# A three-layer f32 network on one core: the last block's mixer changed from column-major to row-major projections, with its entry norm, head norms, rotation and gates rebuilt around that

## What is computed

```python
x = rms_norm(x, final_norm_g)                                   # end of the first block
mod = silu(c) @ w_ada + b_ada                                   # six rows of 1024
shift_m, scale_m, gate_m, shift_f, scale_f, gate_f = split(mod)
h = _rms(x) * (1 + scale_m) + shift_m
proj = h @ w_in     # fq fk fv fog (512 columns each), forget logits (8), rq rk rv rg (512 each)
fq, fk = _rms(fq) * q_gain, _rms(fk) * k_gain                   # by head, 8 heads of 64
fox = softmax(fq fk^T / 8 + cum[t] - cum[s], causal) @ fv       # cum: running sum of log_sigmoid(forget)
fox = _rms(fox) * fox_gain * sigmoid(fog)
rq, rk = _rope(rq), _rope(rk)                                   # 4 heads of 128
ret = (rq rk^T * decay) @ rv
ret = _rms(ret) * ret_gain * silu(rg)
x = x + gate_m * (concat(fox, ret) @ w_out)
h = _rms(x) * (1 + scale_f) + shift_f
x = x + gate_f * (square(relu(h @ w_mlp_in)) @ w_mlp_out)
```

## Time and profile before

| | us |
|---|---|
| median of 3 runs (1222.89 to 1227.58) | 1227.35 |
| the profiled execution | 1228.55 |
| its span | 1226.7 |
| PE busy (95% of the span) | 1167.2 |
| DVE busy (59%) | 720.6 |
| ACT busy (43%) | 525.3 |
| mean granted TensorE clock, share of full | 0.963 |

### The profile page before, as it was taken

How to read it: one execution, slowest core, us unless ns; L and a number is a source line. 1 busy time by engine, 2 the same in 40 slices (tenths; PEclk the granted TensorE clock), 3 DMA queues, 4 the chain that set the end, 5 groups by cost and what they waited for, 6 DMA issues and landing times.

```text
span 1226.7 us, 16582 instructions
## 1 busy us (share of the span) xinstructions
PE 1167.2 (95%) x7264; PEld 1044.9 (85%) x7264; DVE 720.6 (59%) x675; ACT 525.3 (43%) x578; POOL 43.9 (4%) x85
## 2 busy tenths in 40 slices
PE   6988999999999999999999999959989989999998
PEld 4977799898998999989888998849866877898997
DVE  4654465497666776665367667664335566745544
ACT  5544364353544453344454443434332334544441
POOL 2200000000000000000000000010000000000000
PEclk9989899999999999999999999968979889999999
DMA  9832454357577555555447577633122202454540
GB/s 358 311 141 82 152 182 164 136 189 294 211 285 289 212 220 178 201 178 183 167 161 294 215 275 277 235 105 138 70 103 103 69 35 103 173 206 171 188 155 35
DMA packets 31463, 222.12 MB, mean 181 GB/s; under 512 B 3628, under 2 KB 3920, under 8 KB 6688
## 3 DMA queue, kind: packets, MB, share of 16 engines
q1 hardware_dynamic: 26640, 188.03, 42.0%
q0 software_dynamic: 4224, 31.88, 7.2%
q10 hardware_dynamic: 528, 1.16, 0.3%
HBM read 220.01 MB, written 1.05 MB: 180 GB/s over the span
## 4 chain that ended last, share of the span: by engine, by line
PE 87%; DVE 6%; ACT 4%; issue 1%; POOL 0%; DMA 0%; POOLq 0%; ACTq 0%; DVEq 0%
PE ps L426 40%; PE ps L441 38%; ACT hi L968 2%; DVE lo L1382 2%; PE ps L501 1%; PE ps L819 1%; PE ps L816 1%; PE ps L559 1%; PE ps L549 1%; DVE hn L1422 1%; ACT hn L994 1%; PE ps L784 1%; PE ps L665 1%; PE ps L686 1%; DVE work L1857 1%
## 5 line engine op out<-in xcount | busy, mean ns | idle before, releaser
L1382 DVE TENSOR_TENSOR lo<-raw,hi 128x2048 fp32r<-128x2048 f32 x175 | 400.5, 2290 | 246.5 <-ACT hi L968 246.3
L968 ACT ACTIVATE hi<-raw 128x2048 fp32r<-128x2048 f32 x175 | 334.4, 1912 | 360.5 <-PE ps L426 175.1
L426 PE MATMUL ps<-xt_hi,hi 128*128 128x256 f32 x1280 | 367.4, 287 | 6.0 <-DVE xt_lo L1432 6.0
L426 PE MATMUL ps<-xt_hi,lo 128*128 128x256 f32 x1280 | 365.6, 286 | 0.0
L426 PE MATMUL ps<-xt_lo,hi 128*128 128x256 f32 x1280 | 365.4, 285 | 0.0
L426 PEld LDWEIGHTS ps<-xt_hi,hi 128*128 128x128 f32 x1280 | 249.4, 195 | 7.2 <-issue 6.6
L426 PEld LDWEIGHTS ps<-xt_hi,lo 128*128 128x128 f32 x1280 | 249.3, 195 | 0.8 <-issue 0.2
L426 PEld LDWEIGHTS ps<-xt_lo,hi 128*128 128x128 f32 x1280 | 249.1, 195 | 0.0
L441 PE MATMUL ps<-hi,yt_hi 128*128 128x512 f32 x544 | 214.7, 395 | 1.8 <-DVE yt_lo L1628 1.4
L441 PE MATMUL ps<-lo,yt_hi 128*128 128x512 f32 x544 | 212.3, 390 | 0.0
L441 PE MATMUL ps<-hi,yt_lo 128*128 128x512 f32 x544 | 212.3, 390 | 0.0
(11 more groups left out here) (228 smaller groups left out, 1158.1 us busy)
## 6 DMA issues: line engine op xcount, KB each, us to landing
raw<-in_weights SPq DMA_DIRECT2D x176, 1024.0 KB, 5.0
work<-in_w_ada POOLq DMA_DIRECT2D x16, 1536.0 KB, 6.8
work<-in_gains POOLq DMA_DIRECT2D x6, 512.0 KB, 4.1
work<-in_gains ACTq DMA_DIRECT2D x2, 512.0 KB, 7.2
h<-in_x SPq DMA_DIRECT2D x2, 512.0 KB, 6.1
work<-in_mem POOLq DMA_DIRECT2D x2, 512.0 KB, 8.6
work<-in_pool SPq DMA_DIRECT2D x1, 1024.0 KB, 16.4
out_y<-h SPq DMA_DIRECT2D x4, 256.0 KB, 2.0
```

What stands on the lines that cost most here:

```text
L426: mm = pe.matmul(o, ws[:, slot, k, j * P:(j + 1) * P], xs[:, c, :], start=(c == 0 and n == 0 and j % 2 == 0), stop=(c == KC - 1 and n == 2 ...
L968: act.activation(hi[:, p % RING], raw[:, p % RING], ACT.Copy).then_inc(hi_ready, 1)
L1382: dve.tensor_tensor(lo[:, p % RING], raw[:, p % RING], hi[:, p % RING].bitcast(F32), ALU.subtract)\
```

## The change

It reorders the units (fk ahead of fq) and makes all eight projections `unit_x`.

- **Entry norm.** Per tile: add, `gained` (h times the final gain) and `gained_scaled` (times `scale_m`) on DVE, squares of both `h` and the gained row on ACT, five POOL instructions for two roots, and one DVE step by halves (`mix2_rows`) that gives the modulated norm straight from them. The final-normed `h` is written later by ACT. Transposes and `fk` go by tile.
- **Head norms.** ACT squares from the PSUM bank, DVE sums along the row (128x512 to 8 or 4 values), POOL adds eps and raises to -1/2, DVE multiplies the bank by it. The softmax is not divided: the row total enters the eps of the fo norm instead.
- **Forget gate.** 24 matmuls of 256 columns with a padded 128-column weight; the running sum goes as a 65th feature into `k_aug`, against a 65th feature of ones in `q_aug`. Both are then transposed by PE (32 transposes, 65 rows out) and copied.
- **Scores.** One f32 matmul on 65 partitions a head and half of the queries, and then the mask; six groups instead of four. Values come out with rows on the partitions.
- **Rotation.** DVE multiplies by tables of cos, sin and -sin from the bank (four instructions a tile); PE then transposes rq and rk (16).
- **Gates.** ACT's Sigmoid and Silu; `foxg` and `retg` are multiplied into the weights of `out2` when those are split (four instructions a half on ACT and DVE).
- **Rows of mod.** Two transposes of 24 rows (`mod_turn`), a store to DRAM and six loads that repeat a row over the partitions, on POOL's queue.
- **mlp2's norm.** DVE multiplies by `scale_f` ahead of the root and does the rest in one instruction.

"late" is a new 4096-column tile in the place of `mt_hi` and `mt_lo`.

```diff
+    ("fk", _blocks("in2", [1])),
     ("fq", _blocks("in2", [0])),
-    ("fk", _blocks("in2", [1])),
...
+    k_aug, q_aug = late[:, 0:1040], late[:, 1040:2080]
...
-        def row(name, index, first):
-            for j in range(2):
-                o = claim(first + j, ("row", name, j))
-                for k in range(HC):
-                    m = index * KC + j * HC + k
-                    mm = pe.matmul(o[:, k * P:(k + 1) * P],
-                                   mod[:, m:m + 1].to_broadcast((P, P)), ident[:, :],
-                                   start=True, stop=True, skip_group_check=True)
-                filled_by(mm, ("row", name, j))
+        def mod_turn(n, b):
+            def run():
+                pe.wait_ge(*mod_ready.at(n))
+                o = claim(b, ("mod", n))
+                filled_by(pe.transpose(o[0:24, 0:P], mod[:, 24 * n:24 * n + 24], ident[:, :]), ("mod", n))
...
-        transposes("mix2", 0)
-        transposes("mix2", 1)
-        unit_w(UNIT["fq"], XT, (0, 1), split("mix2"))
...
-        head_back("fq", hn[:, 0, :])
...
+        turn_mix2(0)
+        unit_x(UNIT["fk"], XT, (0, 1), "mix2", {(0, 1): lambda: turn_mix2(1)})
...
+        for c in range(KC):
+            for n, (xs, ws) in enumerate(((xt_hi, ff_hi), (xt_hi, ff_lo), (xt_lo, ff_hi))):
+                mm = pe.matmul(o[:, 0:S], ws[:, 8 * c:8 * c + P], xs[:, c, :], start=(c == 0 and n == 0),
+                               stop=(c == KC - 1 and n == 2), skip_group_check=True)
...
+        unit_x(UNIT["fq"], XT, (2, 3), hooks={(1, 0): forget_turned, (1, 1): forget_sums})
...
+                    o = claim(b + i, ("aug", x, t, i))
+                    for k in range(4):
+                        mm = pe.transpose(o[0:65, k * P:(k + 1) * P], src[:, t, 4 * i + k, :], ident[:, :])
+                    filled_by(mm, ("aug", x, t, i))
...
+        unit_x(UNIT["fv"], XT, (0, 1), hooks={(0, 1): aug_turned("fk", k_aug, 0, 4), (1, 0): aug_turned("fk", k_aug, 1, 6),
+                                              (1, 1): aug_turned("fq", q_aug, 0, 4)})
+        aug_turned("fq", q_aug, 1, 6)()
...
-                    pe.matmul(o, fq_t[r, c, qt * P:(qt + 1) * P], fk_t[r, c, 0:nk], start=True, stop=False,
-                              skip_group_check=True)
-                    pe.matmul(o, ident[0:8, 2 * c + b:2 * c + b + 1].to_broadcast((8, P)), cum_rows[:, 0:nk],
-                              start=False, stop=False, skip_group_check=True)
-                    mm = pe.matmul(p[:, a * S + qt * P:a * S + (qt + 1) * P], ident_bf[:, :],
-                                   mask_bf[:, :], start=False, stop=True, skip_group_check=True)
...
-        rotated("q", rq_t, "rq")
...
+                for i, hd in enumerate(heads):
+                    pe.matmul(o[:, i * nk:(i + 1) * nk], fq_t[0:65, hd, qt * P:(qt + 1) * P], fk_t[0:65, hd, 0:nk],
+                              start=(i == 0), stop=False, skip_group_check=True)
+                for i, hd in enumerate(heads):
+                    mm = pe.matmul(o[:, i * nk + qt * P:(i + 1) * nk], ident_bf[:, :], mask_bf[:, :],
+                                   start=False, stop=True, skip_group_check=True)
...
+        unit_x(UNIT["rq"], XT, (2, 3), hooks={(0, 0): together(fox_scores(0, 4), fox_scores(1, 5)),
+                                              (0, 1): together(fox_scores(2, 6), fox_scores(3, 7)),
+                                              (1, 1): together(fox_scores(4, 4), fox_scores(5, 5))})
...
+        unit_x(UNIT["rk"], XT, (0, 1), hooks={(0, 0): together(fox_turned(0, 6), fox_turned(1, 7)),
+                                              (1, 0): together(fox_values(0, 4), fox_turned(2, 6), fox_turned(3, 7)),
+                                              (1, 1): fox_turned(4, 5)})
...
+        unit_x(UNIT["rv"], XT, (2, 3), hooks={(0, 0): fox_turned(5, 6), (0, 1): fox_values(1, 7), (1, 0): mod_turn(1, 6),
+                                              (1, 1): together(*rq_turned)})
...
+        unit_x(UNIT["fog"], XT, (0, 1), hooks={(0, 1): together(*rk_turned), (1, 0): together(ret_scores(0), ret_scores(1)),
+                                               (1, 1): together(ret_scores(2), ret_scores(3))})
...
+        unit_x(UNIT["rg"], XT, (2, 3), hooks={(0, 1): together(ret_values(0, 4), ret_values(1, 5)),
+                                              (1, 0): mixed_turned["fo", 0], (1, 1): mixed_turned["fo", 1]})
...
-        pair(UNIT["out2"], ((yt_ready.at("fo"),), (yt_ready.at("ro"),)),
-             {(0, 1, 0): lambda: row("gate_m", 2, 6), (0, 1, 1): scale_f,
-              (1, 0, 0): lambda: row("shift_f", 3, 6), (1, 1, 0): lambda: row("gate_f", 5, 4),
...
+        pair(UNIT["out2"], ((read(("mixed", "fo", 0)), read(("mixed", "fo", 1))), ()),
+             {(0, 0, 1): mixed_turned["ro", 0], (0, 1, 0): mixed_turned["ro", 1],
+              (1, 0, 0): late_heads(0), (1, 0, 1): late_heads(1),
...
+            if ORDER[p][0] - UNIT["out2"] in (0, 1):
+                gains = "retg" if ORDER[p][1] else "foxg"
+                for k in range(HC):
+                    ins = act.activation(hi[:, p % RING, k], raw[:, p % RING, k], ACT.Copy, scale=col(gains, k))
...
+            act.activation(late[:, n * NB:(n + 1) * NB], src, ACT.Square, scale=1.0 / 32,
+                           accum_out=fin[:, c:c + 1]).then_inc(*fin_sq.up((x, t, b)))
...
+            act.activation(squares_of(x, t), bank(label), ACT.Square, scale=width ** -0.5)\
+                .then_inc(*head_squared.up((x, t)))
...
+            if n == "mlp2":
+                ins = dve.scalar_tensor_tensor(hn[:, t, :], hn[:, t, :], rstd[:, c:c + 1], shift_f_row,
+                                               ALU.mult, ALU.add)
...
+        def gained(t, b):
+            blk = slice(b * NB, (b + 1) * NB)
+            dve.wait_ge(*read(("u", UNIT["mlp1"] + 14 + b, t)))
+            dve.tensor_tensor(hgn[:, t, blk], h[:, t, blk], gain[:, blk], ALU.mult).then_inc(*hg_ready.up((t, b)))
+        def gained_scaled(t):
+            for b in range(2):
+                dve.wait_ge(*hg_ready.at((t, b)))
+            dve.tensor_tensor(hn[:, t, :], hgn[:, t, :], scale_row, ALU.mult).then_inc(*hs_ready.up(t))
+        def mix2_rows(t):
+            dve.wait_ge(*hs_ready.at(t))
+            dve.wait_ge(*fin_r.at(("2", t)))
+            for b in range(2):
+                blk = slice(b * NB, (b + 1) * NB)
+                dve.scalar_tensor_tensor(hn[:, t, blk], hn[:, t, blk], rstd[:, 16 + t:17 + t], shift_row[:, blk],
+                                         ALU.mult, ALU.add).then_inc(*xn_ready.up((t, b)))
         u = UNIT["mlp1"] + 14
...
+            add_residual(u, b, 0)
+            gained(0, b)
+        gained_scaled(0)
         add_residual(u, 0, 1)
+        gained(1, 0)
+        mix2_rows(0)
         add_residual(u, 1, 1)
-        for j in range(2):
-            dve.wait_ge(*read(("row", "scale_m", j)))
-            dve.wait_ge(*read(("row", "shift_m", j)))
-        scaled_row("mix2", 0, h)
...
+            dve.tensor_reduce(mean_sq[:, 8 * n:8 * n + c], cut(squares_of(x, t), c), AX_X, ALU.add)\
+                .then_inc(*head_mean.up((x, t)))
...
+            r = head_r[:, 8 * n:8 * n + c].rearrange("p (a b) -> p a b", b=1).to_broadcast((P, c, NB // c))
+            dve.tensor_tensor(dst, cut(bank(label), c), r, ALU.mult).then_inc(*free(label))
...
+            cos = cos_m[:, t:t + 1, :].to_broadcast((P, 8, 64))
...
-        step(dve.reciprocal(fog_t, fog_t))
...
-        step(dve.reciprocal(rg_exp_t, rg_exp_t))
...
+            gp.tensor_tensor(r, m, power[:, :].to_broadcast((P, c)), ALU.pow).then_inc(*head_root.up((x, t)))
...
+        def final_roots(t):
...
+            gp.tensor_tensor(rstd[:, 14 + t:15 + t], v1, power[:, :], ALU.pow).then_inc(*fin_r.up(("1", t)))
+            gp.wait_ge(*fin_step.at(("a", t)))
+            gp.wait_ge(*fin_sq.at(("g", t, 1)))
+            gp.tensor_tensor(v2, v2, fin[:, 4 * t + 3:4 * t + 4], ALU.add).then_inc(*fin_step.up(("v2", t)))
+            gp.wait_ge(*fin_step.at(("v2", t)))
+            gp.tensor_tensor(rstd[:, 16 + t:17 + t], v2, power[:, :], ALU.pow).then_inc(*fin_r.up(("2", t)))
...
+        gp.wait_ge(mod_stored, 32)
+        gp.dma_start(scale_f_row, mod_row(4)).then_inc(loaded["scale_f"], 16)
+        gp.dma_start(shift_f_row, mod_row(3)).then_inc(loaded["shift_f"], 16)
+        gp.dma_start(gate_f_row, mod_row(5)).then_inc(loaded["gate_f"], 16)
```

955 lines of the change are left out of this document (544 added, 411 removed).

## The result

The changed kernel takes **1132.88 us** (median of 4 runs, 1132.57 to 1133.13), the kernel before, beside it on the same chip, 1225.87. The ratio is 0.924, with a 95% interval of 0.922 to 0.927: 93.0 us less. What came true is nearly to the number the rival that had been given 10% ("all doors in time and no slow clock", 1135).

The account below looks back on a forecast made before the run. The prediction took PE as the bound, with its work, clock and waits. Savings of 36.1 work, 21.2 idle, 22.6 clock and 2 outside the stage sum to 81.9: 1227.35 - 81.9 = 1145.5 us, range 1134 to 1161.

Parts of the forecast that it names:

- all doors in time and no slow clock: First rival listed, 10%: idle 3.5 us, half clock 1 us, second row's cover not missed, 1135 us.
- The work of PE: In the changed stage, PE's work at full clock falls from 177.5 to 141.4 us, by 36.1.
- the lower of its two bounds: 65-row score matmul taken at 0.22 and 0.43 us; the upper bound, 0.41 and 0.62, would add 3.0 us.
- The clock's term: In the changed stage, the half clock's cost falls from 28.6 to 6 us, giving back 22.6.
- perhaps two stretches behind values and scores at 1.7 each: Half-clock loss kept in the changed stage behind values and scores, part of the 6 us kept.
- The waits' term: In the changed stage, PE's idle time falls from 28.7 to 7.5 us, by 21.2; 3.5 stays at the entry.
- three doors and the hand-overs: Idle of 4 us behind the entry: `forget_turned` 0.5, `pair(out2)` 1.1, rows of mod 1, some loss at each hand-over.
- the second covered the chain from the add to the transposes, ... so up to 1.7 comes back as a wait: In the cross attention, two rows removed save 3.4 us of work, but up to 1.7 returns as waiting: gain 2.
- DVE as the bound in bursts: Rival, 20%: DVE holds back units and hooks in the stage, 8 + 4.6 us over the forecast, 1158 us.
- the 1.5 us named as the mark of being wrong: Sign against the forecast: POOL's root of eight values taking over 1.5 us in the profile.
- the clock would not recover: Rival, 7%: low clock follows transposes and f32 pieces, so 20 of the 22.6 us are lost, 1166 us.
- the slower case at 1281: Rival, 2%: pieces put into every unit keep the clock at half through the whole stage, 1281 us.

Follow-up runs that it names:

- score_split: The changed kernel with its 65-row score matmul split into 64 rows and one row, each head's mask behind them, head after head: 1158.93 us.
- before_filled: The kernel before with dummy bf16 matmuls in TensorE's nine waits in the mixer stage: 1218.05 us, ratio 0.992.
- before_grouped: The kernel before with each group's score matmuls ordered by kind (64 rows, then 8 rows, then masks): 1214.09 us, ratio 0.989.
- after_holes: The changed kernel with five waits of about 2 us put into TensorE, at the start of rq, rk, rv, fog and rg: 1143.59 us.
- score_alternate: The changed kernel with each mask set right behind its head's 65-row score matmul, instead of scores first and then masks: 1136.35 us.
- dve_plus2: The changed kernel with sixteen dummy reductions on DVE, two at a time at eight places from fk to the end of rg: 1145.69 us.
- score_split_grouped: The changed kernel with score matmuls split into 64 rows and one row, ordered by kind across heads, then the masks: 1148.00 us.

## Why the prediction was right, and where it fell short

**The work of PE was right.** 36.1 forecast, 35.8 measured. The 65-row score matmul was taken at the lower of its two bounds, 0.22 and 0.43 us, and that held. The timeline of PE, two groups of two heads with 256 keys, answers to the earlier trace rows:

```profile
844.96 1.03 PE L880 MATMUL ps<-work 65*128 65x256 f32 x4
845.83 0.28 PE L883 MATMUL ps<-mask_bf,ident_bf 128*128 128x128 bf16 x2
845.94 1.08 PE L880 MATMUL ps<-work 65*128 65x256 f32 x4
```

Two heads take 845.94 - 844.96 = 0.98 us, masks and all, and score_split shows the upper bound to be the price of the other form (1.41 a head).

**The clock's term was mis-sized: 6 us were kept, 1.7 were lost.** The failed step is "perhaps two stretches behind values and scores at 1.7 each": none came, and "the entry, some 3 us" came to 1.7. The prediction named both causes, the waits and the thin matmuls, but did not price them apart. The runs did: filling the waits is worth 11.6 us of the clock (before_filled), the order of the scores 10.0 (before_grouped); and in the changed kernel neither a wait of 1.8 us amid full matmuls (after_holes) nor a 65-row matmul next to a mask (score_alternate) costs any clock. With that known, 1 to 2 us was the value to take.

**The waits' term was mis-sized too: 7.5 kept, 3.4 left.** At the entry 3.5 was forecast and 0.51 + 1.95 measured. The chain that was walked is the one that is there, with POOL's slow instruction in it. POOL's timeline at the entry, to be read beside the earlier trace rows:

```profile
789.66 1.36 POOL L2183 TENSOR_SCALAR fin<-fin 128x1 f32<-128x1 f32 x1 [7.39 <-ACT late L1330]
...
795.86 0.30 POOL L2183 TENSOR_SCALAR fin<-fin 128x1 f32<-128x1 f32 x1 [2.97 <-ACT late L1330]
```

The same instruction takes 0.30 us for the second tile and 1.36 for the first, where DVE's L1905 runs beside it from 789.63 to 790.86: 1.1 us, and 1.2 had been added. That is the rule of the Trainium skill ("SBUF — State Buffer", Who interferes with whom), and the trace agrees. What was too long lay ahead of the root: it was there 4.1 us after the second add in place of 5.0. From the norm's first half to `xt_lo` 3.4 was walked and 3.3 measured, so the tail was right; the first transposes were busy for 1.32 us and not 0.85, which takes the rest off the wait. Behind the entry 4 us were kept for three doors and the hand-overs. Only `pair(out2)` made PE wait, 0.95 us where 1.1 was forecast. `forget_turned` did not (0.5 forecast), nor did the rows of mod (1 forecast), whose transfers landed after 5.9 us and not 10.3. The loss at each hand-over was nothing at all: PE did not wait once from 797 to 917. The allowance without a row behind it, about 1.4 us, had no place.

**Outside the stage the chain was taken as fixed: 1.7 us were held back, none came.** The step "the second covered the chain from the add to the transposes, ... so up to 1.7 comes back as a wait" failed. The 0.16 us ahead of the transposes of mlp1 were read as the end of a chain that the row just covered. The row was on that chain, through ACT's copy of it, and took 2.2 us of it along when it left (5.3 to 3.1 us). So the rows' whole 3.4 us were gained. In front of mlp2 the forecast was 0 and 0.9 was gained, within its bounds.

**The rivals.** DVE as the bound in bursts had 20%. One of its signs came: POOL's root of eight values is dear, over the 1.5 us named as the mark of being wrong. The trace of line L2217 (ns, least, median and most), and who waits for it:

```profile
L2217 POOL TENSOR_TENSOR late<-late,power x8: 1036/1667/1935, 811.1 to 912.6; 128x8 f32<-128x8 f32 x6, 128x4 f32<-128x4 f32 x2
...
  DVE late L1951: 7.9, 4
  DVE work L1951: 7.2, 4
```

DVE stood 15.1 us at it in eight times, and PE never: DVE's slack swallowed it, as dve_plus2 measured. A mark like that should have been set on PE's waits, not on the length of an instruction off the path. That the clock would not recover, and the slower case at 1281, did not come near: 0.99 against the 0.62 at which it decides. The likeliest case should have been the first rival. Its three numbers (waits 3.5, clock 1, no cover missed) each proved right within 1 us, the last of them by luck, since neither case saw that the chain would shorten. The forecast had taken a cautious figure for each of three uncertain terms and added them up, and all three missed to the same side.

**What stays open.** Why matmuls on few rows bring the clock down is not shown, only that they do, that an order which changes rows does it more, and that no wait is needed that the profile would show. The Trainium skill ("TensorE: Matmul & The Clock Gate", A second HAM failure mode: psum-queue depth-cycling) tells of a clock that falls when TensorE stands still for very short times between groups of matmuls. The busy column can't deny that: it is full while the records of the earlier trace rows stand 0.21 us apart, in place of 0.11. How the 3.4 us of clock in the scores of score_split_grouped share out between its one-row and its 64-row matmuls was not tried. The parts of the change that make up most of the 36 us of work (head sums, their spreading and the rows of mod taken off PE, 20.5 us by the prediction's count) were not undone one by one; their sum is what the windows show.

## What to carry to other kernels

Read the clock and the waits of TensorE apart: a window in which PE is busy all the time and the clock is under 1 points to matmuls on part of the rows or on a few columns, and the cure is there (fold the extra rows into one matmul, order by row count), while a long wait that can't be removed can be filled with dummy matmuls over the full array, here for 6 us. Before work is counted as the cover of a wait, look whether the chain behind that wait starts in this work, as ACT's copy did here. An engine off the path can be loaded until its first door closes, so price it by its slack at each door and not by its share. And where several terms have each a cautious and a plain value, the plain ones together are a case of their own that deserves the weight of a forecast.

## What the chip showed unexpectedly

- The granted clock fell to one half while PE was busy for 41.00 of 41.00 us (score_split, mean 0.67). Five lone waits of 1.8 us did not touch it (after_holes, 0.99).
- f32 matmuls on 64 rows, two on the lower half of the array and then two on the upper (before_grouped), left eight records that start in pairs 0.013 us apart, all in 873.21 - 872.56 = 0.65 us. The eight on 8 rows behind them took 1.09, and so did eight on 64 rows that all stand on the same half (score_split_grouped).
- A power of -0.5 on POOL took 0.55 us for 128x1 (the changed kernel's entry) and a median of 1.67 for the tiles of eight and four values.
- The first 213 us, the same instructions of PE in both kernels, differ by 2.6 us between them with the length of the half-clock stretches (17.1 and 10.2 us). With the waits there filled the stretches were gone.
